# Projections of two mixers computed inside the stages that use them, and the first load of x moved

## The reference

```python
def na_mixer(x, w_in, rpb, mem_k, mem_v):                  # layer 0
    h = x @ w_in                                           # 1024 x (3*768 + 256)
    q, k, v, q_mem = jnp.split(h, [NA_W, 2 * NA_W, 3 * NA_W], axis=-1)
    y = neighbourhood_attention(q * NA_DH ** -0.5, k, v, rpb)   # 12 heads of 64, grid of 16 rows x 64
    return concatenate([y, memory_attention(q_mem, mem_k, mem_v)])

def mlstm_mixer(x, w_in, conv_w, conv_b, w_qkv, gate_b, ...):   # layer 1
    xm, z, gates, q_mem = jnp.split(x @ w_in, [ML_W, 2 * ML_W, 2 * ML_W + 4 * ML_HEADS], axis=-1)
    xc = silu(conv5(xm) + conv_b)                          # over tokens, per channel, 768 channels
    q, k = xc_h @ w_qkv[0], xc_h @ w_qkv[1] * ML_DH ** -0.5     # 4 heads of 192
    v = xm_h @ w_qkv[2]
    ...                                                    # gates give i and log_sigmoid(f)
```

## Time and profile before

| | us |
|---|---|
| median of three runs (7196.35 to 7215.94) | 7209.05 |
| the profiled execution, as timed | 7192.42 |
| its span, first to last instruction | 7190.7 |
| start, loads | 0 to 25.7 |
| memory keys | 25.7 to 69.9 |
| projections of layer 0 (naqk, nav, namq) | 69.9 to 399.8 |
| neighbourhood attention | 399.8 to 753.3 |
| projections of layer 1 (mlx, mlz, mlg, mlmq) | 1807.6 to 2099.4 |
| mlstm_inputs | 2099.4 to 2306.3 |

### The profile page before, as it was taken

How to read it: one execution, slowest core, us unless ns; L and a number is a source line. 1 busy time by engine, 2 the same in 40 slices (tenths; PEclk the granted TensorE clock), 3 DMA queues, 4 the chain that set the end, 5 groups by cost and what they waited for, 6 DMA issues and landing times. The chain is left out here.

```text
span 7190.7 us, 96667 instructions
## 1 busy us (share of the span) xinstructions
PE 5583.1 (78%) x39146; PEld 3021.5 (42%) x39146; DVE 2353.0 (33%) x3955; ACT 1171.5 (16%) x1922; POOL 292.2 (4%) x302
## 2 busy tenths in 40 slices
PE   6877758985856646689959998989928999776787
PEld 3434343332334643433325446888814444222243
DVE  1046330003012664300035265555543121343332
ACT  0024200001002001000013132222211111332201
POOL 0000000001000000000010000000000000121100
PEclk9989869997978877699978999999959999888988
DMA  3121126544123332264442224323141122357731
GB/s 120 58 75 37 71 90 255 214 182 166 53 59 107 99 109 105 79 264 184 179 166 56 74 93 120 67 53 68 42 158 38 36 73 73 126 201 273 263 120 62
DMA packets 578222, 838.88 MB, mean 117 GB/s; under 512 B 179224, under 2 KB 324248, under 8 KB 577368
## 3 DMA queue, kind: packets, MB, share of 16 engines
q1 hardware_dynamic: 509496, 652.45, 27.3%
q0 software_dynamic: 28768, 105.92, 4.1%
q10 hardware_dynamic: 39616, 75.51, 2.9%
HBM read 983.07 MB, written 221.90 MB: 168 GB/s over the span
## 5 line engine op out<-in xcount | busy, mean ns | idle before, releaser
L623 PE MATMUL op_acc<-op_w,op_m 128*128 128x512 f32 x1024 | 453.5, 604 | 60.4 <-DMA op_w<-in_w_out 60.4
L158 PE MATMUL hi_acc<-xT,hi_w 128*128 128x512 f32 x1024 | 445.2, 594 | 6.7 <-DMA hi_w<-in_odd_w_in 6.7
L623 PEld LDWEIGHTS op_acc<-op_w,op_m 128*128 128x128 f32 x1024 | 196.8, 194 | 303.7 <-issue 241.9
L158 PEld LDWEIGHTS hi_acc<-xT,hi_w 128*128 128x128 f32 x1024 | 193.2, 191 | 240.9 <-issue 233.8
L158 PE MATMUL ri_acc<-xT,ri_w 128*128 128x512 f32 (+1 forms) x576 | 257.4, 606 | 10.9 <-DMA ri_w<-in_even_w_in 10.9
L158 PE MATMUL di_acc<-xT,di_w 128*128 128x512 f32 x512 | 224.7, 597 | 7.8 <-DMA di_w<-in_even_w_in 7.8
L3332 PE MATMUL le_gp<-le_g,xT 128*128 128x512 f32 x512 | 220.9, 592 | 0.0
L1105 PE MATMUL moe1e_g_ps<-moe1e_wg,moe1e_xb 128*64 128x512 f32 x768 | 177.6, 616 | 30.9 <-DMA moe1e_wu<-in_exp_w_up 24.0
L1105 PE MATMUL moe0e_g_ps<-moe0e_wg,moe0e_xb 128*64 128x512 f32 x768 | 173.1, 604 | 22.4 <-DMA moe0e_wu<-in_exp_w_up 15.4
L1124 PE MATMUL moe0e_y_ps<-moe0e_wd,moe0e_hT 128*64 128x512 f32 x768 | 180.9, 626 | 7.8 <-ACT moe0e_hT L1172 7.2
L1190 DVE TENSOR_SCALAR moe0e_y<-moe0e_y_ps,moe_weight 128x512 f32<-128x512 f32 x48 | 36.0, 750 | 457.4 <-DMA scratch_y_rows<-moe0e_y 440.7
(11 more groups left out here) (683 smaller groups left out, 8950.4 us busy)
## 6 DMA issues: line engine op xcount, KB each, us to landing
moe0e_wg<-in_exp_w_gate SPq DMA_DIRECT2D x48, 2048.0 KB
moe0e_wu<-in_exp_w_up SPq DMA_DIRECT2D x48, 2048.0 KB
moe0e_wd<-in_exp_w_down SPq DMA_DIRECT2D x48, 2048.0 KB
moe1e_wg<-in_exp_w_gate SPq DMA_DIRECT2D x48, 2048.0 KB
moe1e_wu<-in_exp_w_up SPq DMA_DIRECT2D x48, 2048.0 KB
moe1e_wd<-in_exp_w_down SPq DMA_DIRECT2D x48, 2048.0 KB
op_m<-scratch_mixedT SPq DMA_DIRECT2D x32, 512.0 KB, 9.4
op_w<-in_w_out SPq DMA_DIRECT2D x32, 512.0 KB, 10.4
```

The lines of the kernel that those rows point to most:

```text
L158: mm = pe.matmul(self.acc[i % 2][0:n, h * BANK:(h + 1) * BANK], self.wbuf[i % 3][:, k, 0:n], self.rhs[:, k, h * BANK:(h + 1) * BANK], star ...
L623: mm = pe.matmul(acc[:, n % AHEAD, h * BANK:(h + 1) * BANK], m[:, k, n * P:(n + 1) * P], wb[:, k, h * BANK:(h + 1) * BANK], start=(k == 0) ...
```

## The change

**Start.** The stage "start" is gone. `memory_keys` now loads `ident` ahead of its weights, and `xT` and two small constants behind them, on the same queue; it ends when both its own work and those loads have ended. `x_tm` is loaded in the attention stage.

**Layer 0.** The three projection stages are gone. The attention stage has 20 weight tiles of 128 features: q, k, v of pair 0, then of pair 1 and so on, then two of memory queries. Three weight buffers and one accumulator `acc` of two banks hold them. The tiles of pair 0 are multiplied ahead of the steps. Those of pair j+1 are cut into 4 pieces each and put at the end of TensorE's iterations 0 to 3, 5 to 8 and 10 to 13 of pair j. ScalarE copies a finished tile (1024 columns) at n = 4, 9 and 14, straight into the next pair's `q`, `k` or `ve`; `vo` is made from `ve` by two DMAs from on-chip memory to on-chip memory. v tiles are made with 128 columns per matmul, 64 matmuls a tile. Pairs follow each other without the three emptying iterations, and all loops are written out.

```diff
                 sp.dma_start(m[:], mem.rearrange("(n p) d -> p n d", p=P)).then_inc(m_loaded, 16)
                 sp.dma_start(gb[:, 0, :], g.rearrange("(a d) -> a d", a=1).to_broadcast([P, D])).then_inc(m_loaded, 16)
                 sp.dma_start(gb[:, 1, :], b.rearrange("(a d) -> a d", a=1).to_broadcast([P, D])).then_inc(m_loaded, 16)
+                sp.dma_start(ident[:], ident_in).then_inc(w_loaded, 16)
                 sp.dma_start(w[:], w_kv.rearrange("(k p) f -> p k f", p=P)).then_inc(w_loaded, 16)
+                for out, src in beside:
+                    sp.dma_start(out, src).then_inc(beside_loaded, 16)
                 sp.wait_ge(kept, 1)
...
+                sp.wait_ge(beside_loaded, 16 * len(beside))
...
+                def load_w(i):
+                    if i >= 3:
+                        sp.wait_ge(products, i - 2)
+                    sp.dma_start(wbuf[i % 3][:], tiles[i]).then_inc(w_loaded[i % 3], 16)
...
+                def shift_v(j):
+                    sp.wait_ge(projected, 3 * j + 3)
+                    ve, vo = ves[j % 2], vos[j % 2]
+                    sp.dma_start(vo[0:GW], ve[GW:P, 0:NT - 1, :]).then_inc(vo_loaded[j % 2], 16)
+                    sp.dma_start(vo[GW:P], ve[0:GW, 1:NT, :]).then_inc(vo_loaded[j % 2], 16)
...
+                for i in range(3):
+                    load_w(i)
...
+                load_bias(0)
+                sp.dma_start(x_tm[:], x_in).then_inc(x_loaded, 16)
+                shift_v(0)
+                for j in range(PAIRS):
+                    for i in range(3 * j + 3, min(3 * j + 6, len(tiles))):
+                        load_w(i)
+                    if j + 1 < PAIRS:
+                        load_bias(j + 1)
+                    if j >= 1:
+                        store(j - 1)
+                    if j + 1 < PAIRS:
+                        shift_v(j + 1)
...
-                                                       pt[:, b, j, h * GW:(h + 1) * GW], start=(j == 0), stop=(j == 3))
-                                mm.then_inc(outs, 1)
+                def project(i, piece):
+                    kind, wt = i % 3, wbuf[i % 3]
+                    if piece == 0:
+                        pe.wait_ge(w_loaded[i % 3], 16 * (i // 3 + 1))
+                        pe.wait_ge(projected, i)
+                    for u in range(piece * KD // PIECES, (piece + 1) * KD // PIECES):
+                        if kind < 2:
+                            for h in range(T // BANK):
+                                mm = pe.matmul(acc[:, h * BANK:(h + 1) * BANK], wt[:, u, :], xT[:, u, h * BANK:(h + 1) * BANK],
+                                               start=(u == 0), stop=(u == KD - 1))
+                        else:
+                            for k in range(KD):
+                                mm = pe.matmul(acc[:, u * P:(u + 1) * P], xT[:, k, u * P:(u + 1) * P], wt[:, k, :],
+                                               start=(k == 0), stop=(k == KD - 1))
+                    if piece == PIECES - 1:
+                        mm.then_inc(products, 1)
...
+                for g in range(STEPS + 3):
+                    if g < STEPS:
+                        score(g)
+                    if 0 <= g - 2 < STEPS:
+                        turn(g - 2)
+                    if g >= 3:
+                        mix(g - 3)
+                    j, n = divmod(g, R)
+                    for kind in range(3):
+                        i = 3 * (j + 1) + kind
+                        if i < len(tiles) and 0 <= n - BEGIN[kind] < PIECES:
+                            project(i, n - BEGIN[kind])
...
+                def keep_projection(i):
+                    act.wait_ge(products, i + 1)
+                    out = place(i)
+                    act.activation(out[:].rearrange("p n q -> p (n q)") if i % 3 == 2 else out[:], acc[:], ACT.Copy).then_inc(projected, 1)
...
+                for i in range(3):
+                    keep_projection(i)
+                for g in range(STEPS):
+                    b = g % 2
+                    act.wait_ge(maxima, g + 1)
+                    act.activation(e[:, b, :], e[:, b, :], ACT.Exp, bias=nm[:, b:b + 1], accum_out=rs[:, b:b + 1]).then_inc(exps, 1)
+                    if g >= 1:
+                        keep(g - 1)
+                    j, n = divmod(g, R)
+                    for kind in range(3):
+                        i = 3 * (j + 1) + kind
+                        if i < len(tiles) and n == BEGIN[kind] + PIECES:
+                            keep_projection(i)
...
+        fm = [(h, which, e) for h in range(HEADS) for which in range(2) for e in range(2)]
+        tm = [(hh, c) for hh in range(2) for c in range(NC)]
+        PER_SLOT = 3
+
+        def fm_of(n):
+
+            h = (n - 3) // 2
+            return [4 * h + i for i in range(4)] if n % 2 == 1 and 0 <= h < HEADS else []
+
+        def tm_of(n):
+            first = (n - 10) * PER_SLOT
+            return range(first, min(first + PER_SLOT, len(tm))) if n >= 10 else []
...
+                sp.dma_start(wgate[:], w_v[:, :, G0:M0]).then_inc(g_loaded, 16)
+                rows.load(sp, 0)
+                sp.dma_start(gb[:], gate_b.rearrange("(a f) h -> a (f h)", a=1).to_broadcast([P, 4 * HEADS])).then_inc(g_loaded, 16)
+                sp.dma_start(tr[:], tri).then_inc(g_loaded, 16)
+                sp.dma_start(cw[:], conv_w).then_inc(c_loaded, 16)
+                sp.dma_start(cb[:], conv_b).then_inc(c_loaded, 16)
+                rows.load(sp, 1)
+                rows.load(sp, 2)
                 for m in range(3):
                     sp.dma_start(w[:, m], w_qkv[m].rearrange("h (j d) e -> d h j e", d=QC)).then_inc(w_loaded, 16)
...
+            @block.gpsimd
+            def _(pool):
+                for n in range(N):
+                    for i in fm_of(n):
+                        h, which, e = fm[i]
+                        pool.wait_ge(q_copied, 2 * i + 2)
+                        dst = (qT_out, kT_out)[which].rearrange("(i p) t -> i p t", p=QC)[2 * h + e]
+                        pool.dma_start(dst, qo[:, i % 2, :]).then_inc(q_stored[i % 2], 16)
+                    for i in tm_of(n):
+                        hh, c = tm[i]
+                        pool.wait_ge(t_copied, 2 * i + 2)
+                        for m, dst in ((0, kx_out), (1, vx_out)):
+                            pool.dma_start(dst[c * P:(c + 1) * P, hh * 2 * DH:(hh + 1) * 2 * DH], to[:, i % 2, m, :]).then_inc(t_stored[i % 2], 16)
...
+                for n in range(N):
+                    rows.multiply(pe, n)
+                    if n == 0:
+                        pe.wait_ge(g_ready, 2)
+                        for d in range(2):
+                            pe.matmul(bp[:, d, 0:NC * HEADS], tr[:, d, :], lf[:, d].rearrange("p n h -> p (n h)"), start=True, stop=True)
+                        pe.matmul(bp[:, 2, 0:2 * NC * HEADS], tr[:, 2, :], lf[:].rearrange("p d n h -> p (d n h)"), start=True, stop=True).then_inc(sums, 1)
+                    if fm_of(n):
+                        pe.wait_ge(w_loaded, 48)
+                    for i in fm_of(n):
+                        h, which, e = fm[i]
+                        pe.wait_ge(silu, 2 * h + 2)
+                        for half in range(T // BANK):
+                            pe.wait_ge(q_copied, max(2 * i + half - 1, 0))
+                            for j in range(2):
+                                mm = pe.matmul(qp[0:QC, half, :], w[:, which, h, j, e * QC:(e + 1) * QC],
+                                               xc[:, 2 * h + j, half * BANK:(half + 1) * BANK], start=(j == 0), stop=(j == 1))
+                            mm.then_inc(q_done, 1)
+                    for i in tm_of(n):
+                        hh, c = tm[i]
+                        if i == 0:
+                            pe.wait_ge(silu, NT)
+                            pe.wait_ge(ab_ready, 1)
+                        for m in range(2):
+                            pe.wait_ge(t_copied, max(2 * i + m - 1, 0))
+                            for h in (2 * hh, 2 * hh + 1):
+                                for j in range(2):
+                                    src = xc[:, 2 * h + j, c * P:(c + 1) * P] if m == 0 else xm[:, 2 * h + j, PAD + c * P:PAD + (c + 1) * P]
+                                    mm = pe.matmul(vp[:, m, (h % 2) * DH:(h % 2 + 1) * DH], src, w[:, 1 + m, h, j, :],
+                                                   start=(j == 0), stop=(j == 1))
+                            mm.then_inc(t_done, 1)
...
-        transfer(nc, "start", [(ident[:], I["ident"]), (eye64[:], I["eye64"]), (blk16[:], I["blk16"]),
-                               (x_tm[:], rows(I["x"])), (xT[:], rows(I["xT"]))])
-        memory_keys(nc, I["mem"], I["mem_ln_g"], I["mem_ln_b"], I["w_mem_kv"], ident, mem_kT, mem_v)
-
-
-        w = I["na_w_in"]
-        na_qkT, na_v = dram("na_qkT", 2 * NA_W, SEQ), dram("na_v", SEQ, NA_W)
-        product(nc, "naqk", xT, w[:, 0:2 * NA_W], na_qkT)
```

(16 more changed lines are left out.)

405 lines of the change are left out of this document (206 added, 199 removed).

## The result

The changed kernel takes **6987.36 us** (median of four runs, 6981.41 to 6989.38) where the kernel before, on the same chip, took 7208.74 (7196.35 to 7215.94): ratio 0.9696, 95% interval 0.9685 to 0.9708. The forecast was 6947, the range 6900 to 6995. The sign and the range hold, the range by 8 us only; the point is 40 us too low. The profiled execution took 6989.38, its span is 6987.6.

The account below looks back on a forecast made before the run. TensorE, busy 78% of the span, was taken as nearly full within steps, with slack at loads, stage borders and mLSTM inputs. Gains 24.9 (start) + 97.8 (attention) + 138.8 (mLSTM inputs) = 261.5 took 7209.05 to 6947 us, range 6900 to 6995.

Parts of the forecast that it names:

- Start: Start and memory keys: the load of x is covered by VectorE's and TensorE's work; gain 24.9 us.
- First scores: Attention's opening: first landing, three projection tiles, copy waits and lower clock come to 50.5 us.
- Step 0's wait for weights: Attention's first step: tile 3's load queues behind the shift of v and its copy; 6.2 us.
- A step with a piece: Attention: 2.37 + 3.43 = 5.80 us of TensorE work, VectorE's chain hidden beneath; 68 steps, 394.4 us.
- Copy waits: Attention, n = 5 and 10: new tile waits for ScalarE's copy, about 1.0 us, 11 times, 11.0.
- Pair starts: Attention, pairs 1 to 5: weight loads queue behind the shift of v; 4.1 us each, 20.5.
- The clock behind them: Attention, pairs 1 to 5: the idle gap lowers TensorE's clock; 2.5 us each, 12.5.
- mLSTM inputs: mLSTM inputs with their projections: 498.7 us become 359.9, gain 138.8, TensorE alone late next.
- Rival 1: Attention's pair starts: no waits for weights and the clock holds; 39 us more gain, 6908; chance 0.13.
- Rival 2: Attention's v tiles: weight loads show, half hidden +41 us, 6988; chance 0.06.
- Rival 3: Attention steps: VectorE's chain and the piece add up instead of overlapping; +44 us, 6991; chance 0.07.
- Rival 4: Attention's dense steps: gaps keep the clock at its lower level; +435 us, 7382, slower than before; chance 0.01.

Follow-up runs that it names:

- e4_place: Changed kernel with the projection piece between the transposes and the products with v in TensorE's order, not behind both; 6994.84 us, ratio 0.9721.
- e7_between: e6_copy with pieces 1 to 3 of each projection tile between scores and transposes, piece 0 left at the iteration's end; 6921.73 us, ratio 0.9616.
- e6_copy: e1_wfirst with ScalarE's copy of a finished projection tile ahead of its copy of the transposes; 6929.36 us, ratio 0.9628.
- e1_wfirst: Changed kernel with the attention stage's three weight loads issued ahead of the shift of v on SP's queue, not behind it; 6945.92 us, ratio 0.9653.
- e9: Changed kernel with mlstm_inputs and its four projection stages as before, start and layer 0 as changed; 7085.17 us, ratio 0.9845.
- e12: The kernel before, unedited, executed once more to look at its two memory-attention stages; single time 7203.63 us.
- each part alone: Two kernels against the kernel before: only start and layer 0 changed, 7085.17 us, ratio 0.9845; only layer 1 changed, 7041.59 us, ratio 0.9783.

## Why the prediction was right, and where it was 40 us off

**Start, -24.9.** Right: 24.8. VectorE's first work on the memory rows came at 8.84, behind the landing of the last norm vector; about 8.5 was forecast. The load of x had its cover.

**Attention, 585.6 forecast, 607.8 measured.** Term by term:
1. First scores 50.5 after the stage's first DMA: 50.4 (45.1 to 95.48).
2. Step 0's wait for weights 6.2: measured 6.39.
3. A step with a piece 5.80: measured 6.12, and 6.26 with a v piece. **This is the step that failed**, by 48 x 0.32 + 20 x 0.46 = 24.6 us, more than the stage's whole miss of 22.2; the copy waits and the pair starts give 3.3 back. The prediction named the cost, "up to 0.14" a border and "10 in all", and then took none, "since 0.90, 0.57 and 13.73 hold their borders already". The 0.57 of the transposes did (0.59 measured). But 13.73 / 4 = 3.43 comes from a row in which only projections follow each other, and an interleaved piece has a border at each end: 3.63. And the 0.90 of the scores took 0.17 of drain off 1.08 in a step in which TensorE idled behind the scores, so the row could not show what the next group would cost; start to start they take 1.00. e4_place and e7_between show that a change of width less is 0.08 to 0.10 less; a step has four of them. The v piece's further 0.14 (3.77 for 3.63) is all that can be put down to its weight loads, 32 for 8.
4. Steps without a piece 3.01: as forecast, with the same wait of 0.45.
5. Copy waits 1.0 each: 0.80, 11 times, 2.2 us less. e6_copy shows them to be ScalarE's order and nothing else.
6. Pair starts 4.1 each: 3.48 to 4.32, 19.4 in all for 20.5. e1_wfirst takes them away by moving the loads alone.
7. The clock behind them 2.5 each: the pieces behind the five gaps took 5.16 to 6.43 for 3.70, 10.7 more in all where 12.5 was forecast. Step 0's took 5.64, 1.9 more, for which the sum had nothing. e1_wfirst puts the clock of all six gaps at 11.2.
8. Fill, drain, last store and border were not taken apart; what the other terms leave of the 22.2 is about 1 us.

**mLSTM inputs, 359.9 forecast, 363.8 measured.** The stage behaves as told, the gates at 0.50 for 27.3 us and TensorE then busy nearly throughout. The missing 4 us are at its end. TensorE's last product ends at 2073.5 and the next stage begins at 2084.0, 10.5 us where the sum had 4.6 for the last copy, store and border; the last stores are issued on POOL's queue at 2074.86 and land 2.3 later, and what fills the rest is not shown. Against that, sums and borders took 0.6 where 3 stood: between the groups of this stage, all 96 or 128 wide, a border costs nothing that shows.

**What no step named.** Forecast gains 261.5, in the stages 235.3 by the first pair of profiles, and 228.6 with the attention of the kernel before as its second execution has it (24.8 + 68.9 + 134.9); measured 221. So about 33 of the 40 us lie in the changed stages, 7 of them in a row of the kernel before that was read from one execution only. The 24.5 us in the memory attentions are chance of an execution; single runs of the kernel before went from 7188.74 to 7221.76 beside e9 to e12, at mean clocks of 0.879 and 0.871. An error of this kind cannot be reasoned away; it belongs into the range.

**Rivals.** Rival 1 (no waits, clock holds) did not happen, but e1_wfirst is just that case, made on purpose: 37 of the 39 us that the rival named. Rival 2 (weight loads show in v tiles): a v piece takes 0.14 more than the others, 20 x 0.14 = 2.8 us, and pair 0's v tile 0.7 (14.46 for 13.73), where the rival said 41. The Trainium skill's rule on the gap of back-to-back load-and-multiply pairs ("TensorE: Matmul & The Clock Gate", "Back-to-back issue gap") would have made a v tile 20 us, by the estimate in the prediction; four v pieces in the steps take 15.1, borders included. Rival 3 (pieces do not overlap): its 6.4 a step is not there, and no step with a piece waits for VectorE. The prices of rivals 2 and 3, 6988 and 6991, came close to the 6987 by coincidence, and only the trace tells them apart. Rival 4 (the clock stays down): the stage's clock is 0.97.

## What to carry to other kernels

Price interleaved work with its borders: count in the new order how often TensorE changes between full-width and 64-wide matmuls, since each change taken away gave about 0.1 us back here, which a row of uniform work does not show. When an engine is full, look at who queues ahead of its inputs: moving three weight loads ahead of a waiting DMA gave 37 us, and moving one ScalarE copy ahead of another 10. Before an unchanged stage is explained by a change, run the same code again: here the second execution turned the finding round, and the gain of each part alone held 27 us that did not come from it.

## What the runs showed of the hardware

- The same stage of the same program is granted 1.2 GHz from end to end in one execution (81.9 us) and 2.4 GHz from 17 us into it in another (69.5), with nothing edited.
- The attention's clock stayed up behind eleven waits of 0.80 us, and fell behind eight of eleven of 1.69. A wait that grows by a microsecond so cost up to 2.6.
- The clock also fell, from 1.00 to 0.50, within 64 matmuls of 16 columns (128 records) that had no idle time between them. The Trainium skill ("TensorE: Matmul & The Clock Gate", the table of its two states) names idleness as what brings the lower level back; here that was not needed.
- The order of the same matmuls in a step, with no wait in it, moved the step from 6.12 to 5.92 us: two changes less between full-width and 64-wide work.
